# Banded attention with the values stationary, two heads in two halves of the array's columns, and the probabilities divided before they are turned

## What is computed

```python
def sink_softmax(s, sink):
    sk = sink.astype(jnp.float32)[:, :, None, None]
    m = jnp.maximum(jnp.max(s, axis=-1, keepdims=True), sk)
    e = jnp.exp(s - m)
    return e / (jnp.sum(e, axis=-1, keepdims=True) + jnp.exp(sk - m))
...
    s_band = jnp.where(ok, s_band, -jnp.inf)
    s_ctx = jnp.einsum('bqkgd,bjkd->bkgqj', qblk, kc).astype(jnp.float32) * scale
    p = sink_softmax(jnp.concatenate([s_band, s_ctx], axis=-1), sink_g)
    vv = jnp.concatenate([vb, vc], axis=1)
    return jnp.einsum('bkgqj,bjkd->bqkgd', p.astype(v.dtype), vv)
```

## Time and profile before

| | |
|---|---|
| device time, median of 3 | 1774.96 us (1773.62 to 1777.56) |
| span of the profiled execution | 1773.1 us |
| PE busy | 1735.4 us, 98% of the span |
| DVE busy | 1222.1 us, 69% |
| ACT busy | 803.9 us, 45% |
| POOL busy | 767.4 us, 43% |
| windowed attention, first row maximum to first matmul of the next merge tile | 718.21 to 910.76 us |

### The profile page before, as it was taken

One profiled execution on the slowest core, in us unless ns is written; L12 is line 12 of the kernel. 1 busy time (PEld: TensorE's weight loads), 2 busy tenths in 40 slices (PEclk: granted clock), 3 DMA queues, 4 the chain that ended last, 5 costly groups with the idle time before them and its releaser, 6 DMA issues. The chain is left out here.

```text
span 1773.1 us, 25768 instructions
## 1 busy us (share of the span) xinstructions
PE 1735.4 (98%) x9180; PEld 1478.7 (83%) x9180; DVE 1222.1 (69%) x1720; ACT 803.9 (45%) x1577; POOL 767.4 (43%) x494
## 2 busy tenths in 40 slices
PE   8999999999998999999999999899999999999998
PEld 6997888888887999899988878778888888888887
DVE  3628688879948999688833366875666566575767
ACT  3435333435637888656510145633333333344453
POOL 1407577767533898520022232465555555400000
PEclk9999999999999999999999999999999999999999
DMA  8233233435767665412034242233223323385734
GB/s 349 86 109 137 96 119 155 164 133 190 262 181 199 170 146 146 142 33 72 1 143 160 90 166 87 80 109 117 95 98 126 119 95 128 115 281 201 257 105 178
DMA packets 98567, 249.86 MB, mean 141 GB/s; under 512 B 12321, under 2 KB 26017, under 8 KB 98338
## 3 DMA queue, kind: packets, MB, share of 16 engines
q1 hardware_dynamic: 98466, 248.52, 41.9%
HBM read 183.07 MB, written 65.41 MB: 140 GB/s over the span
## 5 line engine op out<-in xcount | busy, mean ns | idle before, releaser
L750 POOL TENSOR_TENSOR ring<-raw_w,ring 128x512 fp32r<-128x512 f32 x120 | 186.8, 1574 | 138.4 <-ACT ring L621 138.3
L78 PE MATMUL psum<-h_hi,ring 128*128 128x512 f32 x400 | 155.8, 390 | 3.0 <-ACT z L667 2.0
L80 PE MATMUL psum<-h_hi,ring 128*128 128x512 f32 x400 | 155.6, 389 | 0.0
L79 PE MATMUL psum<-h_lo,ring 128*128 128x512 f32 x400 | 155.6, 389 | 0.0
L78 PE MATMUL psum<-u_slot 128*128 128x512 f32 x308 | 120.4, 391 | 1.0 <-DVE u_slot L2953 0.8
L80 PE MATMUL psum<-u_slot 128*128 128x512 f32 x308 | 120.2, 390 | 0.0
L79 PE MATMUL psum<-u_slot 128*128 128x512 f32 x308 | 119.9, 389 | 0.0
L621 ACT ACTIVATE ring<-raw_w 128x512 fp32r<-128x512 f32 x120 | 72.5, 626 | 100.5 <-DVE raw_w L915 32.0
L1406 DVE TENSOR_REDUCE mx<-psum 128x1 f32<-128x1280 f32 x64 | 95.1, 1486 | 9.2 <-PE psum L1292 8.8
L1339 ACT ACTIVATE e<-psum,neg_m 128x1280 f32<-128x1280 f32 x64 | 85.0, 1328 | 31.2 <-DVE neg_m L1407 31.2
L2552 POOL TENSOR_TENSOR cut_lo<-i_raw,cut_hi 128x512 fp32r<-128x512 f32 x44 | 66.8, 1519 | 59.3 <-ACT cut_hi L2407 59.3
(11 more groups left out here) (413 smaller groups left out, 5219.9 us busy)
## 6 DMA issues: line engine op xcount, KB each, us to landing
raw_w<-in_w_pairs SPq DMA_DIRECT2D x40, 512.0 KB, 4.5
qk_dram<-room SPq DMA_DIRECT2D x26, 512.0 KB, 3.6
room<-in_w_ada SPq DMA_DIRECT2D x24, 512.0 KB, 5.3
gates_dram<-ost SPq DMA_DIRECT2D x24, 512.0 KB, 3.0
b_g<-gates_dram SPq DMA_DIRECT2D x8, 1536.0 KB, 7.6
stage<-in_w_ff SPq DMA_DIRECT2D x22, 512.0 KB, 5.9
i_raw<-in_w_ff SPq DMA_DIRECT2D x22, 512.0 KB, 4.9
f_dram<-h SPq DMA_DIRECT2D x22, 512.0 KB, 3.3
```

Source lines behind the costliest of these rows:

```text
L78: pe.matmul(out, sh, mh, start=first, stop=False, skip_group_check=onto)
L79: pe.matmul(out, sh, ml, start=False, stop=False, skip_group_check=onto)
L80: return pe.matmul(out, sl, mh, start=False, stop=last, skip_group_check=onto)
L750: pool.tensor_tensor(w_lo[i], source(p, i), w_hi[i].bitcast(F32), ALU.subtract).then_inc(w_lo_ready, 1)
```

## The change

- The product has the values stationary (128x64) and the turned probabilities moving (128x128). Head 0 writes partitions 0 to 63 of the output, head 1 partitions 64 to 127, and the two alternate tile by tile. The result comes out already transposed, so `out`, its bank in the ring and DVE's `output` fall away; `output_hi` and `output_lo` read the product's bank itself, and `output_lo` is now what releases it. They are done in step i for unit i-2.
- Since the rows of probabilities are now columns, the division by the row sum is done before the turn: `normalise` multiplies the exponentials of a head (128 x 512 or 640, in place, in SBUF) by `rec`. Units 0 to 8 have it on DVE, units 9 to 31 on POOL, and with it the small `sinks`. `turn` waits for it.
- `reciprocals(i)` moves on DVE from the end of the step to just behind the maxima.
- The turned banks are copied whole: the first and third by ACT, the second by DVE (before: first by ACT, the others by DVE in pieces).
- POOL spreads its multiplications `on` over the units; ACT cuts the first merge weights one step earlier, and PE's first merge matmuls are spread anew over the last steps.

```diff
         for i in range(STEPS):
...
-            if 0 <= i - 3 < UN:
-                ring["out", i - 3, 0] = len(ring)
...
             def turn(u):
-                for s in range(2):
-                    pe.wait_ge(exp_done[s], u + 2)
                 for part, todo in enumerate(squares(u)):
                     b, bank = use("turn", u, part)
+                    for s in sorted({s for s, _ in todo}):
+                        pe.wait_ge(norm_ready[s], u + 1)
...
-                b, bank = use("av", u)
-                tiles = tiles_of(u)
-                for s in range(2):
-                    for n, k in enumerate(tiles):
-                        mm = pe.matmul(bank[:, s * HD:(s + 1) * HD], pt[u % 2][:, s, n, :], val[kv][:, k, :], start=(n == 0),
-                                       stop=(n == len(tiles) - 1))
+                b, _ = use("av", u)
+                tiles, out = tiles_of(u), out_of(u)
+                for n, k in enumerate(tiles):
+                    for s in range(2):
+                        mm = pe.matmul(out[s * HD:(s + 1) * HD, :], val[kv][:, k, :], weights_at(u)[:, s * len(tiles) + n, :],
+                                       start=(n == 0), stop=(n == len(tiles) - 1))
                 mm.then_inc(turned[b], 1)
...
                 if i == UN + 1:
+                    first["product"](pe, 0, range(2, BC))
+                if 0 <= i - 2 < UN:
+                    products(i - 2)
+                if i == UN:
                     for s in range(2):
                         pe.wait_ge(exp_done[s], UN + 1)
                     pe.wait_ge(*final("da", GROUPS - 1))
-                    first["product"](pe, 0)
-                if i == UN + 2:
-                    pe.wait_ge(*final("pool", GROUPS - 1))
-                    first["product"](pe, 1, range(2))
-                if 0 <= i - 2 < UN:
-                    products(i - 2)
+                    first["product"](pe, 0, range(2))
...
+        def normalise(eng, u, s):
+            row = e[u % 2][s][:, 0:len(tiles_of(u)) * P]
+            eng.wait_ge(rec_ready, u + 1)
+            eng.tensor_scalar(row, row, rec[:, u % 4, s:s + 1], None, ALU.mult).then_inc(norm_ready[s], 1)
...
+            for u in range(POOL_FROM, UN):
+                sinks(pool, u)
+                for s in range(2):
+                    normalise(pool, u, s)
+                g, rest = divmod(u - 4, 3)
+                if rest == 0 and 2 <= g < GROUPS:
+                    normed(g)
+                if u == UN - 2:
+                    first["pool"](pool, 0)
...
             def output_lo(u):
                 kv, blk, pair = at(u)
-                b, used = slot("out", u)
                 v.wait_ge(yc_hi_ready, u + 1)
                 here = (slice(None), kv * 2 + pair, slice(blk * P, (blk + 1) * P))
-                v.tensor_tensor(y_lo[2][here], banks[4 + b][:, 0:P], y_hi[2][here].bitcast(F32), ALU.subtract).then_inc(free[b], 1)
+                v.tensor_tensor(y_lo[2][here], out_of(u), y_hi[2][here].bitcast(F32), ALU.subtract)\
+                 .then_inc(free[slot("av", u)[0]], 1)
...
+                if i < UN:
+                    reciprocals(ch, i)
+                if i < POOL_FROM:
+                    for s in range(2):
+                        normalise(v, i, s)
                 if 0 <= i - 2 < UN:
-                    output(i - 2)
+                    output_lo(i - 2)
                 if 0 <= i - 1 < UN:
-                    for part in range(1, len(squares(i - 1))):
-                        copy_out(i - 1, part)
+                    copy_out(i - 1, 1)
```

More of the change, by code:

```diff
@@ L1549, in final, with out_of @@
             return free[b], used + 2
-        keep["branches"] = {"rows": final("out", UN - 1), "ring": [last_use(b) for b in range(4)]}
+        def out_of(u):
+            return banks[4 + slot("av", u)[0]][:, 0:P]
+        keep["branches"] = {"rows": final("av", LAST), "ring": [last_use(b) for b in range(4)]}
         def y_part(part, branch, g):
@@ L1728, in _ @@
                     turn_da(DA_STEPS.index(i))
-            first["product"](pe, 1, range(2, BC))
+            pe.wait_ge(*final("pool", GROUPS - 1))
+            first["product"](pe, 1)
             for b in range(2):
                 pe.wait_ge(*last_use(b))
-            pe.wait_ge(*final("out", UN - 1))
+            pe.wait_ge(*final("av", LAST))
         @block.scalar
@@ L1748, in sinks, with copy_out @@
                 act.activation(es[:, u % 2, :], es[:, u % 2, :], ACT.Exp).then_inc(es_ready, 1)
-            def copy_out(u):
-                b, used = slot("turn", u, 0)
+            def copy_out(u, part):
+                if part >= len(squares(u)):
+                    return
+                b, used = slot("turn", u, part)
                 act.wait_ge(turned[b], used + 1)
-                act.activation(pt[u % 2][:, 0, 0:4, :], banks[4 + b].rearrange("p (k n) -> p k n", n=P), ACT.Copy)\
+                out = group(u, part)
+                act.activation(out, banks[4 + b][:, 0:len(squares(u)[part]) * P].rearrange("p (k n) -> p k n", n=P), ACT.Copy)\
                    .then_inc(free[b], 1)
@@ L1838, in _, with normed @@
             pool.wait_ge(rms_ready, 1)
-            for g in range(GROUPS):
+            def normed(g):
                 if g >= 2:
@@ L1869, in reciprocals, with copy_out, output_lo @@
                 ch.link(v.tensor_tensor(sums[:, u % 2, :], sums[:, u % 2, :], es[:, u % 2, :], ALU.add))
-                ch.link(v.reciprocal(rec[:, u % 4, :], sums[:, u % 2, :]))
-            def output(u):
-                b, used = slot("av", u)
+                v.reciprocal(rec[:, u % 4, :], sums[:, u % 2, :]).then_inc(rec_ready, 1)
+            def copy_out(u, part):
+                b, used = slot("turn", u, part)
                 v.wait_ge(turned[b], used + 1)
+                v.tensor_copy(group(u, part), banks[4 + b].rearrange("p (k n) -> p k n", n=P)).then_inc(free[b], 1)
+            def output_lo(u):
+                kv, blk, pair = at(u)
                 if u == 0:
@@ L1930, in _ @@
                     maximum(ch, i, 1)
-                    sinks(i)
+                    if i < POOL_FROM:
+                        sinks(v, i)
                 if i == 3:
@@ L1946, in _ @@
                     v.reciprocal(ss[:], ss[:]).then_inc(rms_ready, 1)
-                if 0 <= i - 3 < UN:
-                    output_lo(i - 3)
-                if i < UN:
-                    reciprocals(ch, i)
-def split_runs(todo):
-    runs = []
-    for n, (s, k) in enumerate(todo):
-        if runs and runs[-1][1] == s:
-            runs[-1][3] += 1
-        else:
-            runs.append([n, s, k, 1])
-    return runs
 def merge_first(nc, sem, banks, keep):
```

70 lines of the change are left out of this document (31 added, 39 removed).

## The result

The changed kernel takes 1784.66 us (median of 4 runs, 1783.72 to 1787.84) against 1774.8 us for the kernel before on the same chip: ratio 1.0058, 95% interval 1.0043 to 1.0072. It is slower, and outside the predicted range of 1767 to 1783. The profiled span is 1781.9 us, 8.8 us more than before.

| stretch | before | forecast | after |
|---|---|---|---|
| first row maximum of unit 0 at | 718.21 | not costed | 718.84 |
| steps 0 and 1 | 14.74 | not costed | 15.74 |
| steps 2 to 8 | 39.10 | 44.3 | **49.15** |
| steps 9 to 30 | 113.04 | 110.2 | 111.66 |
| last unit to the next merge tile | 25.67 | 23.8 | 24.41 |

What follows compares the result with a forecast made beforehand. PE was 98% busy; after the change the chain through DVE and ACT and the late bank were to bound most steps. +5.2 - 2.8 - 1.9 = +0.5 us gave 1775.4 us; own range 1770 to 1780, full range 1767 to 1783.

Steps and rivals of the forecast that it cites:

- Units 2 to 8, divided on DVE: Steps 2 to 8: DVE's two divisions add 0.92 us before the bank's release; 44.3 us against 39.1, 5.2 lost.
- three rivals: Column halves don't overlap (1780.4 us, 0.18); bank isn't late (1757.7, 0.08; milder 1768, 0.14); POOL is slow (1785, 0.10).
- Two halves of the columns: PE's product: the two heads' records overlap, 20 records in 1.1 us instead of 2.17.
- rival without overlap: PE's product: column halves work one after the other, 4.9 us a unit; 5.0 us more, 1780.4 us; chance 0.18.
- The bank that comes free late: Fifth ring use waits for `output_lo`: PE stands 1.3 us; steps with `pool_product` last 5.75 us, with `turn_da` 5.44.
- milder case: Chain 0.25 us shorter in each of 29 steps by closer hand-overs than 0.13: 1768 us; chance 0.14.
- rival 2: Bank isn't late: the ring's fifth use isn't held, 17.7 us less, 1757.7 us; chance 0.08.
- DVE's and ACT's chain: Units 9 to 31: DVE waits for the exponentials within the step; a plain step lasts 4.45 us.
- POOL's division is hidden: Units 9 to 31: POOL's `normalise`, 1.1 us each, two a step, is hidden by scores and products.
- slow-POOL rival: POOL's divisions take 1.97 us each, making a 5.1 us loop; about 10 us more, 1785 us; chance 0.10.
- The end: Last unit to the next merge tile: work before the merge's matmuls falls from 9.2 to 7.3 us, 1.9 saved.

Runs made afterwards that it cites:

- experiment 3: Changed kernel without POOL's four additions and multiplications on the two modulation rows (128x1024): 1780.36 us, ratio 1.0028 to the kernel before.
- experiment 5: Changed kernel with DVE's sum done as two instructions, one per head, the other addend a per-partition scalar: 1790.78 us, ratio 1.0082 to the kernel before.
- experiment 6: Changed kernel with useless matmuls filling PE's idle time in steps 4, 5 and 7: 1781.93 us, ratio 1.0037 to the kernel before.
- experiment 1: Changed kernel with `output_hi` between ACT's two exponentials and `output_lo` ahead of DVE's reciprocals: 1771.77 us, ratio 0.9979 to the kernel before.
- experiment 4: Changed kernel with the probabilities of units 0 to 8 not divided by the row sum: 1779.07 us, ratio 1.0018 to the kernel before.
- experiment 2: Changed kernel with the product's matmuls head after head instead of alternating: 1784.44 us, ratio 1.0046 to the kernel before.
- without POOL's division (7): Changed kernel with the probabilities of units 9 to 31 not divided by the row sum: 1777.60 us, ratio 1.0006 to the kernel before.

## Why the prediction was wrong

**The step that failed** is "Units 2 to 8, divided on DVE": 44.3 us forecast, 49.15 measured, and within it what stands ahead of the bank's release and behind it. The release was put at 4.92 us into the step. In step 5 it came at 6.36 (753.32 to 759.68), because the sum took 1.66 us for 0.16; from there to the next row maximum 2.76 us were forecast and 4.43 measured (to 764.11), because PE's clock had fallen. That makes the 3.1 us of step 5; the held sum of step 6 makes its 1.5. None of the three rivals had such a wait. The division itself was sized right: 0.55 us an instruction and 1.02 for two (forecast 0.53 and 0.92), and experiment 3, which takes the hold out of steps 5 and 6, finds them at 7.59 and 5.32 for 7.7 and 5.37.

What the forecast left out is that `reciprocals` and the division were moved to a place at which POOL works on two SBUF rows, with the bank, the copy and the maximum behind them. Before, the same work of POOL ran in steps 5 and 6 too, and the sum at the step's end just missed it: POOL's instruction ended at 754.29 and the sum started at 754.38.

```profile
751.90 2.39 POOL L1832 TENSOR_TENSOR gate_row<-gate_row,rows 128x1024 f32<-128x1024 f32 x1
754.38 0.15 DVE L1869 TENSOR_TENSOR wsums<-wsums,wes 128x2 f32<-128x2 f32 x1
```

A row that shows the hold was there in DVE's timeline before, and I did not read it:

```profile
728.02 1.64 DVE L1863 TENSOR_TENSOR wes<-wneg_m,wa_sink 128x2 f32<-128x2 f32 x1
```

It ended at 729.66, with POOL's multiply of 128x1024 beside it (727.74 + 1.90 = 729.64); the same operation took 0.16 us in step 2 and 0.20 in step 5. Experiment 3 takes the hold out of steps 5 and 6 (4.7 us there, 3.6 net), experiment 5 moves it, experiment 6 shows the clock as its second price (1.6 us in step 5), and experiment 1 makes it harmless in step 5 by letting the bank go first, though not in step 6. Steps 0 and 1, which I gave nothing, lost 1.0 us: there the divisions take up to 2.12 us beside POOL's operations. Without them the two steps took 14.85 us (experiment 4), with them 15.04 to 16.09 in the profiles of the other experiments, so that the size of this loss is uncertain. The start of unit 0, 0.6 us later, is within its spread over the experiments (717.67 to 719.53).

**Two halves of the columns**: right. 1.24 us to the turn's start, where 1.1 and a change of shape of 0.09 were forecast. The rival without overlap was priced at 5 us; experiment 2 shows that it would have cost nothing (three steps 15.74 us with and without it): PE had that time to spare.

**The bank that comes free late**: right in mechanism and place. PE waits for `y_lo` ahead of `pool_product`, `turn_da` and the row sums, and early release wins 13 us. Which step is which is read from these rows, the other work and DVE's next row maximum of head 0:

```profile
836.58 0.50 PE L78 MATMUL psum<-y_hi,pool_w_hi 128*128 128x512 f32 x1
838.28 0.82 DVE L1888 TENSOR_REDUCE wmx<-psum 128x1 f32<-128x640 f32 x1 [1.16 <-PE psum L1643]
...
847.15 0.63 PE L1678 MATMUL psum<-ident,on 128*128 128x128 f32 x4 [0.23 <-DVE y_lo L1912]
848.52 0.82 DVE L1888 TENSOR_REDUCE wmx<-psum 128x1 f32<-128x640 f32 x1 [0.92 <-PE psum L1643]
```

| step, units 20 to 28 | before | forecast | after | without POOL's division (7) |
|---|---|---|---|---|
| plain | 5.28 | 4.45 | 4.49 | 4.26 |
| `turn_da` | 5.04 | 5.44 | 5.74 | 5.25 |
| `pool_product` | 5.67 | 5.75 | 5.51 | 5.51 |

Without POOL's division all three kinds are some 0.2 us under the forecast, so it is the chain that was put too long, by nearly the 0.25 us of the milder case of rival 2. PE's wait, forecast at about 1.3 us, is 0.60 ahead of `pool_product`; ahead of `turn_da` it is 1.04 to 1.14 without POOL's division, and with it mostly 0.23, since PE has waited for POOL before.

**DVE's and ACT's chain**: right in kind. The plain step without POOL's division is 4.26 us, for 4.45.

**POOL's division is hidden**: wrong. It was sized at 1.1 us and takes 1.89 for 640 columns and 1.56 for 512:

```profile
L1843 POOL TENSOR_SCALAR we<-we,wrec x46: 1564/1886/1892, 787.4 to 900.8; 128x640 f32<-128x640 f32 x34, 128x512 f32<-128x512 f32 x12
L1843 DVE TENSOR_SCALAR we<-we,wrec x18: 546/553/2117, 723.6 to 782.5; 128x640 f32<-128x640 f32 x14, 128x512 f32<-128x512 f32 x4
```

That is above the 1.65 us from which the slow-POOL rival was to decide, and near the upper bound of 1.97; its absence is worth 6.4 us in steps 9 to 30. Yet the forecast of that stretch was only 1.5 us off, 110.2 for 111.66, and the plain step of 4.49 lies beside the forecast 4.45. The forecast was 0.24 us too high for `pool_product` and 0.3 too low for `turn_da`. Two errors cancelled: a chain 5 us too long and a division 6.4 too cheap. That was luck: a sum that comes out is no proof of its terms. Likewise the rival's 1785 us is the measured time, but in steps 9 to 30 it asked for 120, and there were 111.66: right number, wrong place.

**The end**: 24.41 for 23.8, the right sign, 1.3 of the 1.9 us.

One reading of the prediction is slightly off and nothing rests on it: the 16.0 us of three steps before are 5.33 each on average, not 5.27 to 5.3.

## What to carry to other kernels

Before you move a small instruction that reads two SBUF tensors onto a chain that others wait for, look at what POOL runs at that time: here a sum of 128x2 numbers cost 0.16 or 1.66 us by its neighbour alone. When one instruction frees a bank that PE is queued for, put it ahead of everything in its engine's step that nobody waits for as urgently; that reordering was worth 13 us, and it decided which engine the division belonged on. Time that an engine is busy, even 98% of it, may be work that just fills a wait: the same steps took as long with PE at 87%.

## What the runs showed of the hardware

- Two fp32 products with 64 stationary columns each, in different halves of the array's columns and alternating, take 1.24 us for 20 records; head after head they take 1.95 (experiment 2).
- POOL's multiply of 128x640 fp32 by a scalar for each partition takes 1.89 us, 3.4 times DVE's 0.55, and per column (2.9 ns) almost what its operation on two tensors takes, 1574 ns for 512 columns, and not the cast's 609 ns.
- A sum of 128x2 on DVE with two SBUF tensors, started while POOL worked on two SBUF rows, ended when POOL's instruction ended (758.17 and 758.16 in step 5), 1.66 us for 0.16. With a scalar operand in place of the second tensor two of 128x1 were not held (0.34 us for both), but two multiplies of 128x640 were (1.88 us for 1.02), all in experiment 5.
- PE's granted clock was 1.00 up to 757 and 0.55 from 759.6 to 763.4, behind 3.22 us of idle time; with that time filled it was 1.00 (experiment 6). Behind 2.66 us it was 1.00 in one profile and 0.56 in another, at the same place of the same code. The stretches of the changed kernel:

```profile
759.60:763.40 3.80, 3.72 (x6) 1.65 (x7) 0.62 (x2) 0.60 (x2) 0.00 (x0) 0.55 0.00 0
750.00:757.00 7.00, 5.84 (x44) 4.32 (x44) 3.81 (x9) 3.67 (x10) 3.57 (x2) 1.00 0.01 2
```
